# Two gathered transfers at a time: diagonal products on four 64x64 quarters of the array

## The reference, cut to what matters

```
act = gelu(einsum('td,tkd->tk', x, peer_u[eidx]))        # one dot of 1024 per token and pick
y   = einsum('tk,tkd->td', gates * act, peer_v[eidx])    # a sum of 128 rows of 1024 per token
```

## Time and profile before

| | us |
|---|---|
| median of 3 runs (lowest, highest) | 2608.19 (2602.96, 2612.71) |
| span of the profiled execution | 2607.3 |
| PE busy, of the span | 2152.8 (83%) |
| DVE busy | 1647.3 (63%) |
| ACT busy | 1003.4 (38%) |
| POOL busy | 702.4 (27%) |
| first transfer issued, last sum of Y and residual ends | 661.58, 2036.4 |

### The profile page before, as it was taken

How to read it: one execution, slowest core, us unless ns; L and a number is a source line. 1 busy time by engine, 2 the same in 40 slices (tenths; PEclk the granted TensorE clock), 3 DMA queues, 4 the chain that set the end, 5 groups by cost and what they waited for, 6 DMA issues and landing times. The chain is left out here.

```text
span 2607.3 us, 25567 instructions
## 1 busy us (share of the span) xinstructions
PE 2152.8 (83%) x8090; PEld 1334.7 (51%) x8090; DVE 1647.3 (63%) x3381; ACT 1003.4 (38%) x2477; POOL 702.4 (27%) x610
## 2 busy tenths in 40 slices
PE   6999978897878687877868887676777787899998
PEld 6778855676423232322324453232333474788877
DVE  5674266535888988878456776656766555555534
ACT  3213345323443343333334344435533455433322
POOL 0120031000444354443434454444444100000000
PEclk8999988998999899898989999787988897999999
DMA  7664200211899999999999999999999433222222
GB/s 243 218 208 113 67 5 26 77 61 75 340 419 420 400 403 420 396 420 398 415 380 415 414 414 411 420 370 359 420 419 420 159 92 122 91 97 97 80 81 97
DMA packets 142827, 683.18 MB, mean 262 GB/s; under 512 B 19648, under 2 KB 36320, under 8 KB 74224
## 3 DMA queue, kind: packets, MB, share of 16 engines
q0 software_dynamic: 73728, 536.90, 50.3%
q1 hardware_dynamic: 68976, 144.78, 17.0%
HBM read 679.50 MB, written 2.10 MB: 261 GB/s over the span
## 5 line engine op out<-in xcount | busy, mean ns | idle before, releaser
L2483 PE MATMUL peer_Y<-peer_w,peer_diag 128*128 128x512 f32 x1784 | 902.5, 645 | 242.2 <-ACT peer_diag L2469 215.2
L2428 POOL DMA_INDIRECT peer_w<-in_peer_uv,peer_eidx x510 | 606.4, 1189 | 703.7 <-PE peer_Y L2483 465.8
L2437 DVE CUSTOM_DVE_ANT_0 peer_w<-peer_w,peer_xtok 128x1024 f32<-128x1024 f32 x510 | 617.7, 1222 | 198.1 <-DMA peer_w<-in_peer_uv,peer_eidx 195.3
L2483 PEld LDWEIGHTS peer_Y<-peer_w,peer_diag 128*128 128x128 f32 x1784 | 337.8, 202 | 753.2 <-ACT peer_diag L2469 443.7
L2461 ACT ACTIVATE peer_gel<-peer_dots 128x1 f32<-128x1 f32 x512 | 103.8, 203 | 721.8 <-DVE peer_dots L2437 721.5
L2469 ACT ACTIVATE peer_diag<-all_ident,peer_a 128x128 f32<-128x128 f32 x448 | 179.8, 401 | 18.1 <-PE peer_Y L2483 3.6
L2463 ACT ACTIVATE peer_a<-peer_gel,peer_gates 128x1 f32<-128x1 f32 x512 | 150.8, 294 | 16.6
L2992 PE MATMUL m_acc<-m2x_hs,m2x_cut 128*128 128x512 f32 (+1 forms) x384 | 143.7, 374 | 6.4 <-PEq L123 3.7
L2993 PE MATMUL m_acc<-m2x_hs,m2x_cut 128*128 128x512 f32 (+1 forms) x384 | 143.3, 373 | 0.0
L2994 PE MATMUL m_acc<-m2x_hs,m2x_cut 128*128 128x512 f32 (+1 forms) x384 | 143.2, 373 | 0.0
L1293 ACT ACTIVATE p_cut<-m1h_raw 128x512 fp32r<-128x512 f32 (+2 forms) x96 | 58.2, 609 | 202.1 <-PE p_acc L1240 119.3
(11 more groups left out here) (518 smaller groups left out, 3731.2 us busy)
## 6 DMA issues: line engine op xcount, KB each, us to landing
m_gates<-in_w_ada SPq DMA_DIRECT2D x48, 512.0 KB, 4.3
m2x_raw<-in_w_up SPq DMA_DIRECT2D x22, 1024.0 KB, 4.8
m1h_raw<-in_w_in SPq DMA_DIRECT2D x80, 256.0 KB, 3.1
m20h_raw<-in_w_in SPq DMA_DIRECT2D x48, 256.0 KB, 7.3
m22h_raw<-in_w_in SPq DMA_DIRECT2D x48, 256.0 KB, 2.8
m_down_ring<-in_w_down SPq DMA_DIRECT2D x22, 512.0 KB, 3.4
m_out_ring<-in_w_out SPq DMA_DIRECT2D x16, 512.0 KB, 7.8
peer_w<-in_peer_uv,peer_eidx POOLq DMA_INDIRECT x510, 16.7
```

The lines of the kernel that those rows point to most:

```text
L2428: pool.indirect_dma_start(self.slot(n).rearrange("p c n -> p (c n)"), None, self.uv_dram, bass.IndirectOffsetOnAxis(self.col(self.eidx, n) ...
L2437: dve.tensor_tensor_reduce(u, u, self.xtok[:, n // PICKS, :], 1.0, 0.0, ALU.mult, ALU.add, self.col(self.dots, n)).then_inc(self.dotted, 1)
L2483: ins = pe.matmul(self.Y[:, h, :], self.diag[:, i % self.RD, :], self.slot(n)[:, 1, h * BANK:(h + 1) * BANK], start=(k == 0), stop=(i == l ...
```

## The change

The index and gate columns of odd picks are stored with token halves exchanged: partition p < 64 gets the index of token p + 64, and the other way round. So an even transfer is as before, and an odd one brings the rows of the other half's tokens. Its dots are taken with `xrot`, a copy of the tile's `xtok` with halves exchanged, which ACT makes once per tile (two copies of 64x1024). ACT takes gelu of two columns at once, after the odd dot, and nothing else. DVE now makes the matrices: for each transfer of a pair `Z[128, 64]`, which is `halves` (two 64x64 identities on top of each other) times gelu times gate, in step 2 m + 2 for pair m, ahead of that step's dots, with two buffers for Z.

PE multiplies a pair in two turns. In each turn four products of 64 rows and 64 columns of the array run over 512 columns each: even and odd transfer, lower and upper rows. An odd transfer's lower rows belong to upper tokens, so the four products use the four different quarters. In a turn the lower rows write one bank of `Y` and the upper rows the other; in the second turn the banks change places. The second turn waits for the end of the first (`crossed`), and the first turn of the next pair for the end of the second (`used`).

The fold on DVE, `a`, `diag` and the identity scaling are gone. A slot is free when its pair's second turn is done. The limit in `fetch_to` is now the largest n whose pair's step lies before the step given. The projection's weight ring beside the gather goes from six buffers to five.

```diff
@@ TopK.vector, last stage
-            dve.scalar_tensor_tensor(self.eidx[:, t, ks], e[:, 0, ks], float(NKEYS), e[:, 1, ks], ALU.mult, ALU.add)
-            ins = dve.tensor_tensor(self.gates[:, t, ks].rearrange("p (h k) -> p h k", h=n), self.ex[:, hs], bc(self.rden[:, hs], 2, K), ALU.mult)
+            for at, rows, odd in ((slice(0, P), slice(0, P), 0), (slice(0, 64), slice(64, P), 1), (slice(64, P), slice(0, 64), 1)):
+                own = slice(h0 * K + odd, (h0 + n) * K, 2)
+                dve.scalar_tensor_tensor(self.eidx[at, t, own], e[rows, 0, own], float(NKEYS), e[rows, 1, own], ALU.mult, ALU.add)
+                ins = dve.tensor_tensor(self.gates[at, t, own].rearrange("p (h k) -> p h k", h=n), self.ex[rows, hs, odd:K:2],
+                                        bc(self.rden[rows, hs], 2, K // 2), ALU.mult)
@@ Gather.fetch_to, fetch
-        self.fetch(pool, min(self.N, step + self.RW - 3))
+        limit = self.fetched
+        while limit < self.N and (limit < self.RW + len(self.lent) or (limit - self.RW) // 2 * 2 + 2 < step):
+            limit += 1
+        self.fetch(pool, limit)
...
-                pool.wait_ge(*self.consumed(n - self.RW))
+                pool.wait_ge(self.used, (n - self.RW) // 2 + 1)
@@ Gather.vector
+        m = s // 2 - 1
+        if s % 2 == 0 and 0 <= m < self.N // 2:
+            dve.wait_ge(self.gelued, m + 1)
+            if m >= 2:
+                dve.wait_ge(self.used, m - 1)
+            for j in range(2):
+                gates = self.gates[:, m * 2 // PICKS, (2 * m + j) % PICKS:(2 * m + j) % PICKS + 1]
+                ins = dve.scalar_tensor_tensor(self.Z[:, m % 2, j, :], self.halves[:], self.col(self.gel, 2 * m + j), gates.to_broadcast([P, 64]), ALU.mult, ALU.mult)
+            ins.then_inc(self.spread, 1)
...
+            if k == 1:
+                dve.wait_ge(self.turned, 2 * t + 2)
-            dve.tensor_tensor_reduce(u, u, self.xtok[:, n // PICKS, :], 1.0, 0.0,
+            x = self.xrot[:] if n % 2 else self.xtok[:, t, :]
+            dve.tensor_tensor_reduce(u, u, x, 1.0, 0.0, ALU.mult, ALU.add, self.col(self.dots, n)).then_inc(self.dotted, 1)
...
-            dve.scalar_tensor_tensor(y, self.slot(n)[:, 1, :], self.col(self.a, n), y, ALU.mult, ALU.add).then_inc(self.folded, 1)
@@ Gather.turn_rows (new), scalar
+        if t:
+            act.wait_ge(self.dotted, t * PICKS)
+        for r in range(2):
+            act.activation(self.xrot[64 * r:64 * r + 64, :], self.xtok[64 - 64 * r:P - 64 * r, t, :], ACT.Copy).then_inc(self.turned, 1)
...
+        if n % 2:
+            k = n % PICKS
+            pair = lambda x: x[:, n // PICKS % 2, k - 1:k + 1]
+            act.wait_ge(self.dotted, n + 1)
+            act.activation(pair(self.gel), pair(self.dots), ACT.Gelu).then_inc(self.gelued, 1)
@@ Gather.tensor
+        for turn in range(2):
+            if turn == 1:
+                pe.wait_ge(self.crossed, m + 1)
+            elif m >= 1:
+                pe.wait_ge(self.used, m)
+            for j in range(2):
+                for r in range(2):
+                    h, half = (r + turn) % 2, (r + j) % 2
+                    rows, out = slice(64 * r, 64 * r + 64), slice(64 * half, 64 * half + 64)
+                    ins = pe.matmul(self.Y[out, h, :], self.Z[rows, m % 2, j, :], self.slot(2 * m + j)[rows, 1, h * BANK:(h + 1) * BANK],
+                                    start=(k == 0 and turn == 0), stop=(k == PICKS - 2 and turn == 1))
+            ins.then_inc(self.used if turn else self.crossed, 1)
@@ second_front
-ring = Early(ph3.sb("raw", [P, 6 if pacer is not None else KD, BANK], side="right"), ...
+ring = Early(ph3.sb("raw", [P, 5 if pacer is not None else KD, BANK], side="right"), ...
```

More of the change, by code:

```diff
@@ L93, in shape_constants @@
     out["c_ident"] = np.eye(P, dtype=np.float32)
+    out["c_halves"] = np.tile(np.eye(64, dtype=np.float32), (2, 1))
     out["c_iota"] = np.tile(np.arange(P, dtype=np.float32), (P, 1))
@@ L2375, in __init__ @@
         self.lent_landed = [ph.sem(f"lent_landed{r}") for r in range(len(lent))]
-        names = ("dotted", "gelued", "weighed", "diaged", "used", "folded", "added")
-        self.dotted, self.gelued, self.weighed, self.diaged, self.used, self.folded, self.added = (ph.sem(n) for n in names)
+        names = ("dotted", "turned", "gelued", "spread", "crossed", "used", "added")
+        self.dotted, self.turned, self.gelued, self.spread, self.crossed, self.used, self.added = (ph.sem(n) for n in names)
         self.fetched = 0
@@ L2383, in open @@
         self.ring += [ph.sb(f"w{i}", [P, 2, D])[:] for i in range(self.LOW, self.RW)]
-        self.dots, self.gel, self.a = (ph.sb(n, [P, 2, PICKS]) for n in ("dots", "gel", "a"))
-        self.diag = ph.sb("diag", [P, self.RD, P])
+        self.dots, self.gel = (ph.sb(n, [P, 2, PICKS]) for n in ("dots", "gel"))
+        self.xrot = ph.sb("xrot", [P, D])
+        self.Z = ph.sb("Z", [P, 2, 2, 64])
     def slot(self, n):
@@ L2395, in landing @@
         return (self.lent_landed[n], 16) if n < E else (self.landed[(n - E) % self.RW], 16 * ((n - E) // self.RW + 1))
[L2397 to L2406, removed]
     @staticmethod
@@ L2477, in tensor @@
-        pe.wait_ge(self.diaged, i + 1)
-        pe.wait_ge(*self.landing(n))
+        t, k = divmod(2 * m, PICKS)
+        pe.wait_ge(self.spread, m + 1)
         if k == 0 and t >= 1:
             pe.wait_ge(self.added, 2 * t)
-        last = self.products((t + 1) * PICKS) - 1
-        for h in range(2):
-            ins = pe.matmul(self.Y[:, h, :], self.diag[:, i % self.RD, :], self.slot(n)[:, 1, h * BANK:(h + 1) * BANK],
-                            start=(k == 0), stop=(i == last))
-        ins.then_inc(self.used, 1)
@@ L2488, in pick @@
-def pick(nc, gather, top, qT, keys, mod, rows, steps):
-    ident = gather.consts["ident"]
+        for j in range(2):
+            pe.wait_ge(*self.landing(2 * m + j))
+        for turn in range(2):
[3 more added lines that the diff above has]
+                pe.wait_ge(self.used, m)
+            for j in range(2):
+                for r in range(2):
[4 more added lines that the diff above has]
+            ins.then_inc(self.used if turn else self.crossed, 1)
@@ L2491, in pick @@
+def pick(nc, gather, ident, top, qT, keys, mod, rows, steps):
     FAST, PACES = 112, (3, 2)
@@ L2621, in peer_and_front @@
             gather.open()
-            pick(nc, gather, top, qT, tables["keys"], mod, kept.rows, STANDALONE)
+            pick(nc, gather, consts["ident"], top, qT, tables["keys"], mod, kept.rows, STANDALONE)
         pacer = Pacer(gather, STANDALONE)
```

46 lines of the change are left out of this document (13 added, 33 removed).

## The result

The changed kernel takes 2639.38 us (median of 4 runs, 2636.03 to 2641.09), the kernel before 2610.36 in the same comparison: a ratio of 1.0112, 95% interval 1.0092 to 1.0132. The forecast was 2609, its range ended at 2634, and rival B's 2635 was the nearest number. The profiled execution has a span of 2637.2 us, 29.9 over that of before. All ratios compare executions in the chip's usual state; one of the eleven of `smooth_before`, 5297 us, was in another and is left out of its ratio.

What follows compares the result with a forecast made beforehand. The DMA engines were taken to bound the gather. The terms 0.5 + 1 + 3 - 4 + 0 + 1.4 gave +1.9 us on a span of 2607.3, forecast 2609 us; its own range was 2598 to 2621, the 80% range 2592 to 2634.

Steps and rivals of the forecast that it cites:

- rival B: Gather: pairs starve the DMA queue in the pick stretches and the stops from 1325 to 1810; 2635 us, chance 0.14.
- the products at full clock: PE: quarters overlap fourfold, so a pair's two turns take 2.4 us; 7.4 us if nothing overlaps.
- the lower clock: PE in `pick`: the 1.2 GHz level is possible; a pair then takes some 4.5 us, costing hold only.
- the start's first issue: Ahead of the very first transfer: four added index instructions cost 0.5 us, between 0.4 and 0.8.
- the end: From the last dot's start to the last sum: 5.9 us instead of 4.5, +1.4 us.
- the weight ring: Weight loads beside the gather, six buffers to five: costs nothing, at worst 3 us.
- rival A: PE products: the quarters overlap less, so a pair takes 4.8 us; 2680 us, chance 0.06.
- The hold of a slot: Three tile-pick stretches: with slots held longer the queue could run dry earlier; +1 us each, from -1 to +4.
- DVE, "I price this at 1 us": 685 to 885: added matrix pieces shrink DVE's wait to 8 us, DMA stays the bound; 1 us, ends 0 and 8.
- The passage, -4: From `pick` to the second block, at 1325: the new limit allows two more transfers; -4 us, from -6 to 0.
- Behind 320, 0: 1685 to 1810, linear attention and start of the other attention: wider limit, no folds, slower first release; 0, from -10 to +5.
- rival C: Relief counts: passage filled (-6), half of 17 us from 1685 to 1810, catching up (-4); 2592 us, chance 0.18.

Runs made afterwards that it cites:

- smooth_before: The kernel before with the three long stages of a tile's picks on DVE cut into one-head pieces; 2602.96 us, ratio 0.9978.
- pair_hold: The kernel before, with POOL reissuing a slot only when its pair partner's has been used too; 2623.13 us, ratio 1.0055.
- dve_load: The kernel before with two unused 128x64 DVE matrices added per pair, behind a wait for gelu; 2622.6 us, ratio 1.0058.
- hold_and_load: The kernel before with both additions: reissue only when the pair is used, and two unused DVE matrices per pair; 2641.47 us, ratio 1.0125.
- smooth_after: The changed kernel with the three long stages of a tile's picks on DVE cut into one-head pieces; 2620.1 us, ratio 1.0046.
- old_limit: The changed kernel with the fetch limit of the kernel before; 2632.23 us, ratio 1.009.
- z_now: The changed kernel with matrices and products one step earlier, right behind the odd dot; 2648.54 us, ratio 1.0153.

## Why the prediction was wrong

Right were the bound (DMA, not PE), the products at full clock (a pair 2.4 us forecast, 2.27 measured; PE 51.05 of 80 us in 1245 to 1325, about 50 forecast), the lower clock (a pair 4.5 us forecast, 3.8 to 4.1 measured), the start's first issue (+0.5; the first dot doesn't wait for it, 669.32 against 669.30), the end (5.9 us forecast, 6.0 measured: the last dot starts at 2055.42, the last sum ends at 2061.46), the weight ring as far as seen (its loads land in 7.7 us, 7.3 before; it wasn't tried by itself) and rival A's refutation. For A spoke a rule of the Trainium skill ("TensorE: Matmul & The Clock Gate", What overlaps and what doesn't); read as A reads it, a pair would take 4.8 us, and it takes 2.27. The order that the section states holds here (by the profile's ends, which are modelled, no product of `peer_Y` ends before an earlier one); what doesn't is that weight loads overlap only matmuls of another row group: in the pair above four of them start from 1304.18 to 1304.20, while products in both row groups run until 1304.76.

**The hold of a slot failed: "I take +1 us for each of three".** This term holds the largest part of the error: dots 64 to 256 lose 13.8 us where it gave 3. pair_hold, dve_load and hold_and_load put 3.4, 2.7 and 7.5 us on dots 64 to 192, and 1.9, -0.9 and 4.0 on 192 to 256. I weighed the extra hold against the mean landing time of 16.7 us in steady state, and priced the hold and DVE's work as two terms. But in the pick stretches DVE starts no dot for 9 us, and with these pauses cut up in both kernels only 4.1 of the 13.8 us are left (smooth_after against smooth_before). My reading is that of two transfers whose release is held to the pair's end, one is missing from the queue for the whole pause; POOL's longest waits fit it (10.1 us in the kernel before, 12.8 in pair_hold, 14.1 in hold_and_load; in the changed kernel two of 8.6 and 7.9), though the slots weren't counted. The time added to a *mean* hold, 2.3 us, was the wrong measure. Rival B was near throughout: it priced each stretch at 3.8 us (4.6 measured), DVE's full stretch at 5 (3.6 in dots 0 to 64), and the stops from 1325 on at 12 less the 4 of the passage (6.1 behind dot 256).

**DVE, "I price this at 1 us".** DVE is busy 187.6 of 200 us and waits 4.3 us for landings, as forecast, but the rate is 410 GB/s there, not 419. The pieces take 0.48 us a pair (0.24 each) instead of 0.35. That isn't it: with the same pieces dve_load and hold_and_load keep 420 and 419 GB/s and lose nothing in the first 64 dots (+0.1, -0.1). There the products don't wait for the pieces. Where they do, the first 64 dots lose 3.1 to 7.2 us (changed kernel, old_limit, smooth_after, z_now), and with the matrices on ACT 0.2 and 0.3. So for that stretch the load itself was priced about right, and what the term left out is that a slot's release now stands behind DVE's own order of work. 1 us was near the lower end of my range, 0 to 8.

**The passage, -4, is +4.** The two transfers were issued at 1351.77 and 1353.02, as forecast, and 1325 to 1365 reads 417 GB/s, over the 380 named as a sign. But that window lies 18 us too early for this kernel: the last dot of `pick` starts at 1344.88, at 1327.13 before. The window moved with it loses 40 x 111/420 = 10.6 us, against 6.3 before. The two transfers fill its first half, and the hole behind them is deeper:

```profile
1342.70:1382.70 40.00, 18.39 (x92) 5.81 (x88) 21.86 (x49) 8.33 (x19) 12.11 (x12) 0.67 0.79 309
...
1362.70:1382.70 20.00, 11.75 (x63) 2.91 (x61) 16.11 (x35) 4.80 (x12) 7.21 (x6) 0.76 0.57 202
```

What is late next is transfer 267. `pick` ends with step 258, an even transfer; its slot was free alone before (issued at 1349.31, 22.2 us after that dot's start), now it waits through the whole stop for the partner's dot (1372.95, 28.1 us after it):

```profile
1353.02 0.95 POOL L2423 DMA_INDIRECT peer_w<-in_peer_uv,peer_eidx  x1 [0.30 <-issue]
...
1372.95 1.76 POOL L2423 DMA_INDIRECT peer_w<-in_peer_uv,peer_eidx  x1 [11.88 <-PE peer_Y L2491]
```

In pair_hold it is 28.7 us, with +2.6 in the passage. That a stop between the two halves of a pair is the cause is read from these rows; ending `pick` on an odd step wasn't tried, and dve_load, which releases every slot by itself, loses 5.2 us there.

**Missing from the sum: POOL's order.** The limit was priced only where it lets POOL run ahead. It also puts fetches ahead of POOL's share in a norm: 7.3 us read at dot 320, some 4 to 5 that last, by old_limit. The hold reaches the same place (pair_hold).

**Behind 320, 0, is -5.9** in the table, but most of that is the delay of dot 320 being made up; from dot 350 on it is -2.1. pair_hold, with no relief of PE at all, has -2.1 there too, hold_and_load +2.0. So where rival C put its relief, at most some 4 us of it are seen. The 14 us by which hold_and_load is behind the change at dot 350 (22.1 against 8.2) arise earlier, and which part of the change saves them is open.

By terms: dots 0 to 64 3.6 (forecast 1.5, first issue and DVE's full stretch), pick stretches 13.8 (3), passage 4.1 (-4), norm and behind it 2.0 (0), end 1.5 (1.4), not explained 4.8.

**What beats both** is not the change but smooth_before: 2602.96, ratio 0.9978, against 2620.1 for the same edit under the change.

## What to carry to other kernels

When a transfer queue hides an engine's pauses, price a longer hold in the longest pause, not at the mean: count how many slots are free to be reissued while the engine stands still. An engine relieved at 80% busy gave next to nothing here, since the bytes were the bound. Work moved to one at 88% busy cost nothing while the queue was full, 13.7 us in all over the gather (dve_load), and more where the release of slots came to stand behind it. A limit on how far an in-order queue runs ahead is also a limit on what it puts in front of others: look at everything else that engine has to do.

## What the hardware showed that was not expected

- Products on 64x64 quarters overlap even where the two records of one float32 product use the same quarter: 16 records of 512 columns in 2.27 us, a turn of eight in 1.09, as four at a time would take.
- With PE busy about two thirds of the time in `pick` the granted clock was 0.73 instead of 0.98. The same sixteen records then took from 2.27 to 4.06 us. Eight more small products per pair brought 0.96.
- Two 128x64 operations of DVE take 0.48 us in a row, and one lasts 0.28 us by the page's mean; one with 128 columns lasts up to 0.29. Halving a matrix's columns saved little.
